# Four changes together in a two-block transformer kernel: opening order, output projections begun inside the attentions, modulation summed by VectorE, copies of transposes moved up

## The chip, the cores and the metric

One core of one Trainium2 chip. The metric is the device time of one execution in microseconds (us). Lower is better.

## What is computed

Two transformer blocks run one after the other on x (512 tokens, 1024 features, fp32). The first block is a gated feed-forward network, an attention with eight banded heads and eight heads that mix three branches (compressed, selected, windowed), and a second feed-forward network. The second block has two layers, both steered by a condition vector c:

```
c_act = silu(c)
mod = c_act @ mod_w[l] + mod_b[l]                    # 1024 x 6144, for l = 0, 1
sh1, sc1, g1, sh2, sc2, g2 = split(mod, 6)
hn = rms_norm(h, norm1_g[l]) * (1 + sc1) + sh1
h = h + g1 * (attention(hn) @ wo)                    # l = 0: chunked, l = 1: latent
hn = rms_norm(h, norm2_g[l]) * (1 + sc2) + sh2
h = h + g2 * conv_ffn(hn)
...
shift, scale = split(c_act @ kv_mod_w + kv_mod_b)    # 1024 x 2048, between the layers
return rms_norm(h, final_g)
```

So the modulation is one vector of 14 panels of 1024 features: 14 matrices of 1024 x 1024 against the one vector c_act.

## The kernel before

Every large product is made of three fp32r matmuls: activation and weight are each split into a high and a low part (hi, lo), and hi*hi, lo*hi and hi*lo are summed in PSUM (`feature_major` L345 to L347 or with the operands' roles kept the other way L339 to L341). A weight chunk of 128 x 2048 is loaded by SP into `raw` (two slots), ScalarE copies it to `w_hi` (`split_hi`, L318), VectorE subtracts to give `w_lo` (`split_lo`, L322), and TensorE uses it. The semaphore `used` frees the slot of hi and lo, `lo_done` that of `raw`. Order on each engine is the order in which the program text calls its functions; there is no scheduler.

The stages, in order of time: ffn1, projection and `att_1`, output projection `out_1`, ffn2, qkv and `att_chunked`, `out_2`, ffn3, latent layer and `att_latent`, `out_3`, ffn4. Ahead of each stage a `Norm` scales the rows of x on VectorE (L609), transposes them on TensorE (L677) into banks, and ScalarE and VectorE take them out as `xT_hi` and `xT_lo` (L625 and L649, or L632 to L660 where a shift is added).

**Opening.** SP issues two rows, the four parts of x, then some 25 small loads of constants (L372), and then the first weight chunk. ScalarE does the norm's squares, the eight `xT_hi`, then the first `w_hi`. VectorE does the scaling, the eight `xT_lo`, the first `w_lo`, and then the constants out of PSUM (banks 5 and 6, L467). TensorE waits for the last `xT_lo`, transposes the constants (L443 to L446), waits for `cols_done`, and starts ffn1.

**Modulation.** GpSimd loads 1024-column rows of a panel, 512 KB each, in four slots (L530), eight to a panel. VectorE multiplies each by its element of c_act, a value per partition, and sums them in `mod_sum` (L544, L546). Then `mod_reduce` (L555) sums over partitions on TensorE with eight matmuls against a column of ones, and `mod_columns` (L561) adds the bias. Ten panels are made beside ffn1, one for two chunks of weights, and four beside the output part of ffn2. The sum is one panel late, so `mod_reduce` stands 15 times.

**Attention.** `PairAttention.pe` runs steps k. In each it issues the scores of k, the products with the values of k-2, and the transposes of the probabilities of k-1 (L1458, L1498, L1480). VectorE adds bias and takes the minimum (L1594), ScalarE takes the exponentials (L1532), VectorE and GpSimd scale by the inverse sums (L1652), and after the transposes ScalarE and VectorE copy banks 4 to 6 into `score` (L1545, L1547), from where the products with the values read. `copies` names who copies which bank: act, dve, act. On ScalarE the copies stand behind all four exponentials of a step, on VectorE behind the scaling. `values_pe` waits for all copies.

**Output projection.** `MixOut` multiplies the attention's result by w_out in two panels of 512 columns, each from two chunks (kt 0 to 3 and 4 to 7), for four groups of 128 tokens s, in banks 4 to 7 for both panels. In the second block, VectorE multiplies by the gate row g1 (L2000) and adds to x (L2003). `Row` makes such a row: eight transposes on TensorE (L1949) into banks 0 and 1, two copies on VectorE (L1955, L1956) into `row`. `row_g1` (g1) is made behind the attention, and TensorE waits for it; `row_g2` (g2, for ffn3) behind `out_2`, and TensorE waits for that ahead of the norm's transposes. The same holds for `row_g3` and `row_g4` in the second layer. Between the panels of `out_2`, VectorE makes the angles of the rotary tables and ScalarE their sine and cosine (`rope_dve`, `rope_act`).

Of the kernel before, what the change touches and what calls it, by code (L numbers as in the profile page):

```python
# [4 lines left out]
P = 128  # L5
# [82 lines left out]
def program(nc, A, strips_dram, skewed, out):  # L88
    stack = ExitStack()
    with stack:  # L90
# [44 lines left out]
        mod_sum = take("mod_sum", [P, MOD])  # L135
# [3 lines left out]
        row = take("row", [P, D])  # L139
        score = take("score", [P, 4, SEQ])  # L140
        probT_at = cursor[0]
        cT = take("cT", [P, 2, SEQ])
        cols = take("cols", [P, 5 * P + 2 * KT])
        mod_cols = take("mod_cols", [P, 15 * KT])
        ident = take("ident", [P, P])
        mean_w = take("mean_w", [P, P])
        ones = take("ones", [P, 1])
# [3 lines left out]
        c_act = take("c_act", [P, KT])  # L151
# [22 lines left out]
        first_rows = take("first_rows", [2 * KT, P], at=work + 12288)  # L174
# [114 lines left out]
        col["ffn1_norm"], col["c"] = FIRST, FIRST + KT  # L289
# [11 lines left out]
        def mod_part(name):  # L301
            k = PANELS[name] + 1
            return mod_cols[:, KT * k:KT * k + KT]
# [52 lines left out]
        in_dma, x_in, first_in, small_in, c_act_done = sem("in_dma"), sem("x_in"), sem("first_in"), sem("small_in"), sem("c_act_done")  # L356
# [9 lines left out]
        def first_load(sp):  # L366
            for n, name in enumerate(("ffn1_norm", "c_2")):
                sp.dma_start(first_rows[n * KT:(n + 1) * KT, :], by_128(A[name][0])).then_inc(first_in, 16)
# [25 lines left out]
        def constants_load_small(pool):  # L394
# [9 lines left out]
            get(cmp_b2v[:, :], A["cmp_b2"][0, 1].partition_broadcast(P))  # L404

# [28 lines left out]
        def first_pe(pe):  # L434
            pe.wait_ge(ident_done, 2)
            pe.wait_ge(first_in, 32)
            pe.transpose(bank[7][:, 0:2 * KT], first_rows[:, :], ident[0:2 * KT, 0:2 * KT]).then_inc(cols_T, 1)

        def constants_pe(pe):
            pe.wait_ge(in_dma, in_dmas[0])  # L440
            pe.wait_ge(edge_zero, ROWS_MADE)
            for b in range(4):
                pe.transpose(bank[5][:, b * P:(b + 1) * P], rows[:, b, :], ident[:, :])  # L443
            pe.transpose(bank[6][:, 0:P], rows[:, 4, :], ident[:, :])
            for kind in range(2):
                last = pe.transpose(bank[6][:, P + kind * CMP_LEN:P + (kind + 1) * CMP_LEN],  # L446
                                    pos_rows[:, kind, :, :].rearrange("p a d -> p (a d)"),
                                    ident[0:CMP_LEN, 0:CMP_LEN])
            last.then_inc(cols_T, 1)

        def first_dve(dve):
# [4 lines left out]
            dve.memset(ones[:, :], 1.0)  # L456
            for n in range(MOD_SLOTS):
                dve.memset(mod_sum[:, n * MOD // MOD_SLOTS:(n + 1) * MOD // MOD_SLOTS], 0.0).then_inc(mod_step, 1)
            dve.memset(mod_cols[:, :], 0.0)
# [3 lines left out]
            dve.tensor_copy(cols[:, FIRST:FIRST + 2 * KT], bank[7][:, 0:2 * KT]).then_inc(cols_done, 1)  # L463

        def constants_dve(dve):
            dve.wait_ge(cols_T, 2)
            dve.tensor_copy(cols[:, 0:4 * P], bank[5][:, :])  # L467
            dve.tensor_copy(cols[:, 4 * P:5 * P], bank[6][:, 0:P])
            dve.tensor_copy(cmp_pos[:, :, :].rearrange("p a b -> p (a b)"),
                            bank[6][:, P:P + 2 * CMP_LEN]).then_inc(cols_done, 1)  # L470
# [33 lines left out]
        def c_act_act(act):  # L504
            act.wait_ge(cols_done, 1)
            act.activation(c_act[:, :], column("c", KT), ACT.Silu).then_inc(c_act_done, 1)


        mod_step, mod_red, mod_ev = sem("mod_step"), sem("mod_red"), sem("mod_ev")
# [9 lines left out]
        def modulation_pool(pool, first, end, strip=None):  # L519

            p0 = 0
            for w in (A["mod_w_2"][0], A["kv_mod_w_2"], A["mod_w_2"][1]):
                n = w.shape[1] // MOD
                lo, hi = max(first - p0, 0), min(end - p0, n)
                if lo < hi:
                    with pool.Fori(0, hi - lo) as p:
                        for kt in range(KT):
# [3 lines left out]
                                           w[kt * P:(kt + 1) * P, bass.ds(MOD * lo + MOD * p, MOD)]).then_inc(mod_ld[kt % MOD_SLOTS], 16)  # L531
# [5 lines left out]
        def mod_steps(dve, k, kts):  # L537

            for kt in kts:
                dve.wait_ge(mod_ld[kt % MOD_SLOTS], 16 * (KT // MOD_SLOTS * k + kt // MOD_SLOTS + 1))  # L540
                dve.wait_ge(mod_step, KT * k + kt + MOD_SLOTS)
                c = c_act[:, kt:kt + 1]
                if kt == 0:
                    ins = dve.tensor_scalar(mod_sum[:, :], mod_rows(0), c, None, ALU.mult)  # L544
                else:
# [4 lines left out]
        def mod_reduce(pe, k, b):  # L550

            pe.wait_ge(mod_step, KT * k + MOD_SLOTS)
            pe.wait_ge(mod_ev, k + 1)
            for t in range(KT):
                last = pe.matmul(bank[b][:, t:t + 1], lhsT=mod_sum[:, t * P:(t + 1) * P], rhs=ones[:, :],  # L555
                                 start=True, stop=True)
            last.then_inc(mod_red, 1)

        def mod_columns(dve, k, b):
            dve.wait_ge(mod_red, k + 1)  # L560
            dve.tensor_tensor(out=mod_cols[:, bass.ds(KT * k, KT)], in0=bank[b][:, 0:KT],  # L561
                              in1=cols[:, bass.ds(KT * k + (col["mod_b"] - KT), KT)], op=ALU.add).then_inc(mod_ev, 1)
# [11 lines left out]
        class Norm:  # L574
# [36 lines left out]
            def act(self, act, gained=None):  # L611

                if not self.again:
                    for s in range(TOK):
                        self.stats_act(act, s)
                if gained is not None:
# [20 lines left out]
            def dve(self, dve, scaled=0):  # L637

                for s in range(scaled, TOK):
                    self.scale_dve(dve, s)  # L640

# [66 lines left out]
        credited = [used, mod_ev, *pair_free, *x_added]  # L708
# [1981 lines left out]
```

## Time and profile before

| what | value |
|---|---|
| median of 3 runs | 2349.35 us (2349.22 to 2352.9) |
| the profiled execution | 2358.37 us |
| its span | 2356.9 us |
| TensorE busy (matmuls) | 2255.7 us, 96% of the span |
| VectorE, ScalarE, GpSimd busy | 54%, 41%, 12% |
| mean granted TensorE clock | 0.976 of full speed |
| DMA | 266.41 MB, mean 113 GB/s |

A profile row of the timeline gives start, duration, engine, source line, operation, and in brackets how long the engine was idle before it and which instruction released it. Matmuls overlap: one of 512 columns is shown with 0.39 us while the next starts 0.23 us after it.

### The profile page before, as it was taken

Reading aid. Unit: us, or ns where it says so; the run is one execution under the profiler, and the core shown is the slowest. Engines: PE = TensorE matmul, PEld = TensorE weight load, DVE = VectorE, ACT = ScalarE, POOL = GpSimd, SP = SyncE. Lnnn points to the kernel's source line nnn. Section 1 sums busy time; section 2 is a strip of 40 time slices with the busy share of each in tenths; the row PEclk is TensorE's granted clock in tenths of the full one; section 3 lists DMA queues with packets and bytes.
Section 4 is the critical chain, followed back from the end, with each engine's and each line's share of the span. In section 5 each row is a group of like instructions: output and inputs, shape, how many; then the busy total and the mean of one; then the engine's idle time right before and its main releaser. Section 6 shows DMA issues by size and latency. Waiting matters only on the chain.

```text
span 2356.9 us, 31898 instructions
## 1 busy us (share of the span) xinstructions
PE 2255.7 (96%) x11876; PEld 1882.9 (80%) x11876; DVE 1273.7 (54%) x1968; ACT 964.1 (41%) x1469; POOL 275.0 (12%) x441
## 2 busy tenths in 40 slices
PE   6999999998899999999999899999989999999998
PEld 5888887896778888888887778888878877888886
DVE  5763763535744344346338566456466656554564
ACT  4322323425735323324228354245244554542542
POOL 2110220013520011001009000000000340000000
PEclk9999999986999999999999999999999999999999
DMA  6863983212022356345321222332312102333322
GB/s 208 262 220 111 284 300 121 72 56 82 28 90 72 89 184 203 85 155 192 106 91 55 76 72 80 108 107 71 116 47 72 55 19 72 89 94 111 89 86 92
DMA packets 258594, 266.41 MB, mean 113 GB/s; under 512 B 8847, under 2 KB 201918, under 8 KB 258510
## 3 DMA queue, kind: packets, MB, share of 16 engines
q1 hardware_dynamic: 236925, 187.20, 26.7%
q0 software_dynamic: 21584, 78.10, 9.7%
q8 instruction: 51, 0.84, 0.1%
q14 instruction: 34, 0.27, 0.0%
HBM read 263.10 MB, written 12.66 MB: 117 GB/s over the span
## 4 chain that ended last, share of the span: by engine, by line
PE 88%; DVE 5%; ACT 4%; issue 1%; SPq 1%; POOL 0%; DMA 0%; DVEq 0%; ACTq 0%; POOLq 0%
PE bank L339 15%; PE bank L341 15%; PE bank L340 15%; PE bank L345 11%; PE bank L347 11%; PE bank L346 11%; PE bank L1458 2%; PE bank L1480 2%; PE bank L1498 2%; ACT probs L1532 2%; PE bank L555 1%; PE bank L677 1%; DVE xT_lo L652 1%; ACT score L1545 1%; DVE probs L1594 1%
## 5 line engine op out<-in xcount | busy, mean ns | idle before, releaser
L322 DVE TENSOR_TENSOR w_lo<-raw,w_hi 128x2048 fp32r<-128x2048 f32 (+3 forms) x202 | 415.3, 2056 | 388.1 <-ACT w_hi L318 387.6
L339 PE MATMUL bank<-xT_hi,w_hi 128*128 128x512 f32 x1552 | 607.4, 391 | 8.1 <-DVE xT_lo L652 4.2
L340 PE MATMUL bank<-xT_lo,w_hi 128*128 128x512 f32 x1552 | 604.5, 390 | 0.0
L341 PE MATMUL bank<-xT_hi,w_lo 128*128 128x512 f32 x1552 | 604.5, 390 | 0.0
L318 ACT ACTIVATE w_hi<-raw 128x2048 fp32r<-128x2048 f32 (+3 forms) x202 | 348.2, 1724 | 498.9 <-PE bank L347 448.5
L339 PEld LDWEIGHTS bank<-xT_hi,w_hi 128*128 128x128 f32 x1552 | 291.9, 188 | 72.0 <-DVE xT_lo L652 8.1
L341 PEld LDWEIGHTS bank<-xT_hi,w_lo 128*128 128x128 f32 x1552 | 291.8, 188 | 61.4
L340 PEld LDWEIGHTS bank<-xT_lo,w_hi 128*128 128x128 f32 x1552 | 292.0, 188 | 59.7
L345 PE MATMUL bank<-w_hi,hid_hi 128*128 128x512 f32 x704 | 274.3, 390 | 0.0
L347 PE MATMUL bank<-w_hi,hid_lo 128*128 128x512 f32 x704 | 273.9, 389 | 0.0
L346 PE MATMUL bank<-w_lo,hid_hi 128*128 128x512 f32 x704 | 273.9, 389 | 0.0
L1652 POOL TENSOR_SCALAR probs<-probs,stat 128x256 f32<-128x256 f32 (+2 forms) x120 | 120.5, 1016 | 739.7 <-DVE stat L1571 711.2
L841 ACT ACTIVATE hid_hi<-act_u 128x512 f32 (+1 forms) x88 | 55.6, 632 | 292.7 <-DVE act_u L900 292.7
L347 PEld LDWEIGHTS bank<-w_hi,hid_lo 128*128 128x128 f32 x704 | 132.2, 188 | 27.6
L345 PEld LDWEIGHTS bank<-w_hi,hid_hi 128*128 128x128 f32 x704 | 132.2, 188 | 27.3
L346 PEld LDWEIGHTS bank<-w_lo,hid_hi 128*128 128x128 f32 x704 | 132.2, 188 | 27.2
L1532 ACT ACTIVATE probs<-probs,small 128x512 f32<-128x512 f32 (+2 forms) x224 | 120.7, 540 | 78.8 <-DVE small L1594 78.8
L345 PE MATMUL bank<-w_hi,xT_hi 128*128 128x512 f32 (+3 forms) x320 | 113.2, 354 | 3.9 <-DVE xT_lo L652 2.9
L346 PE MATMUL bank<-w_lo,xT_hi 128*128 128x512 f32 (+3 forms) x320 | 112.1, 350 | 0.0
L347 PE MATMUL bank<-w_hi,xT_lo 128*128 128x512 f32 (+3 forms) x320 | 112.1, 350 | 0.0
L892 DVE SCALAR_TENSOR_TENSOR act_u<-bank,cols,act_u 128x511 f32<-128x511 f32 x88 | 65.9, 749 | 78.6 <-ACT act_u L833 72.3
L900 DVE TENSOR_TENSOR act_u<-act_g,bank 128x512 f32<-128x512 f32 x44 | 30.2, 687 | 138.2 <-PE bank L341 138.2
(295 smaller groups left out, 2922.9 us busy)
## 6 DMA issues: line engine op xcount, KB each, us to landing
raw<-in_ffn_w_in_dram SPq DMA_DIRECT2D x40, 1024.0 KB, 6.1
raw<-in_f_win_dram SPq DMA_DIRECT2D x40, 1024.0 KB, 6.0
mod_w<-in_mod_w_dram POOLq DMA_DIRECT2D x48, 512.0 KB, 5.5
mod_w_more<-in_mod_w_dram POOLq DMA_DIRECT2D x48, 512.0 KB, 5.9
raw<-in_ffn_w_out_dram SPq DMA_DIRECT2D x24, 768.0 KB, 4.5
raw<-in_f_wout_dram SPq DMA_DIRECT2D x24, 768.0 KB, 4.4
raw<-in_a_wqkv_dram SPq DMA_DIRECT2D x12, 1024.0 KB, 5.1
skewed_strips<-bias_strips POOLq DMA_DIRECT2D x32, 320.0 KB, 6.5
```

The lines of the kernel that those rows point to most:

```text
L318: act.activation(w_hi[:, slot, :n], raw[:, slot, :n], ACT.Copy).then_inc(hi_done, 1)
L322: dve.tensor_tensor(out=w_lo[:, slot, :n], in0=raw[:, slot, :n], in1=w_hi[:, slot, :n].bitcast(f32), op=ALU.subtract).then_inc(lo_done, 1)
L339: pe.matmul(o, lhsT=w[0], rhs=xs[0], start=first, stop=False)
L340: pe.matmul(o, lhsT=w[0], rhs=xs[1], start=False, stop=False)
L341: return pe.matmul(o, lhsT=w[1], rhs=xs[0], start=False, stop=last)
L345: pe.matmul(o, lhsT=xs[0], rhs=w[0], start=first, stop=False)
L346: pe.matmul(o, lhsT=xs[0], rhs=w[1], start=False, stop=False)
L347: return pe.matmul(o, lhsT=xs[1], rhs=w[0], start=False, stop=last)
L841: act.activation(hid_hi[:, bass.ds(k, 1), :].rearrange("p a n -> p (a n)"), act_u[:, u, :], ACT.Copy).then_inc(hid_hi_done, 1)
L892: dve.scalar_tensor_tensor(out=dst[:, u, shift:], in0=bank[b][:, :SEQ - shift], scalar=w, in1=dst[:, u, shift:], op0=ALU.mult, op1=ALU.add ...
L1532: act.activation(p, p, ACT.Exp, scale=-1.0, bias=self.least(k, i), accum_out=self.sums(k, i)).then_inc(self.e, 1)
L1652: return engine.tensor_scalar(p, p, self.inverses(k, i), None, ALU.mult)
```

## The change

1. **Modulation.** The modulation weights are laid out with features first in the host's arrays, so that a load holds 128 output features (partitions) by 1024 inputs. c is loaded to all partitions (`c_row`) and put through silu there. Each of the eight loads of a panel is one fused multiply and sum along the row on VectorE, which gives 128 features. `mod_sum`, `mod_reduce`, its bank and its waits are gone, and `mod_columns` closes each panel.
2. **Opening.** The first weight chunk is issued ahead of the constants, its split stands between the norm's statistics and `xT_hi` (ScalarE), and between scaling and `xT_lo` (VectorE). The constants' transposes use banks 2 and 3 and wait for four `xT_lo`; only the second chunk waits for `cols_done`.
3. **Attention.** ScalarE copies bank 4 between the second and third exponentials, VectorE copies bank 5 ahead of `lo` and scaling; `values_pe` waits for the banks that the next products read.
4. **Output projection.** The first panel goes to banks 0 to 3. Its first chunk for s = 0 is issued in the attention's step N, for s = 1 in step N+1 (N is the number of steps). Gate rows g1 are made in step 1 of the attention, g2 between the panels, both copied by ScalarE, each into a tile of its own.

```diff
         def mod_steps(dve, k, kts):
             for kt in kts:
                 dve.wait_ge(mod_ld[kt % MOD_SLOTS], ...)
-                dve.wait_ge(mod_step, KT * k + kt + MOD_SLOTS)
-                c = c_act[:, kt:kt + 1]
...
-                    ins = dve.scalar_tensor_tensor(out=mod_sum[:, :], in0=mod_rows(kt), scalar=c,
-                                                   in1=mod_sum[:, :], op0=ALU.mult, op1=ALU.add)
-                ins.then_inc(mod_step, 1)
+                tile = mod_rows(kt)
+                dve.tensor_tensor_reduce(out=tile, in0=tile, in1=c_row[:, :], scale=1.0, scalar=0.0, op0=ALU.mult, op1=ALU.add,
+                                         accum_out=mod_dots[:, kt:kt + 1]).then_inc(mod_step, 1)
 
+            def copied(self, pe, k, b):
+                by = self.steps[k].copies[:b + 1]
+                pe.wait_ge(self.pa, self.after("pa", k, by.count("act")))
+                if "dve" in by:
+                    pe.wait_ge(self.pd, self.after("pd", k, by.count("dve")))
...
                         act.activation(self.hi[:, g, :], bank[7][:, :], ACT.Copy).then_inc(self.h, 1)
+                    if 1 <= k <= len(self.steps):
+                        self.copies(act, k - 1, "act", (0,))
                     if step and step.windows is None:
                         self.exps_act(act, k, (2, 3))
...
+                    large = step and step.windows is None and step.sink is None
+                    if large:
+                        dve.wait_ge(self.e, self.after("e", k, 2))
+                        dve.reciprocal(self.inverses(k, 0, 2), self.sums(k, 0, 2)).then_inc(self.r, 1)
+                    if 1 <= k <= len(self.steps):
+                        self.copies(dve, k - 1, "dve")
                     if k - 2 in self.last:
...
+            def beside(self):
+                k = len(self.att.steps)
+                return {k: lambda pe: self.gemm.piece(pe, 0, 0, [0]), k + 1: lambda pe: self.gemm.piece(pe, 0, 0, [1])}
+            def pe(self, pe, between=None):
+                self.gemm.piece(pe, 0, 0, [2, 3])
+                self.gemm.piece(pe, 0, 1, range(TOK))
+                if between:
+                    between(pe)
+                self.gemm.pe(pe, 1)
...
+                def second_free(pe, p, s):
+                    if s == 0 and self.row_between:
+                        self.row_between.done(pe)
+                    if s == TOK - 1:
+                        att.done(pe)
...
             for s in range(TOK):
                 sp.dma_start(x[:, s, :], ...)
+            ffn1.pair_sp(sp, 0, 0, 0)
             constants_load(sp)
...
-            norm_ffn1.act(act)
-            split_hi(act, 2, 0, landed(2))
+            norm_ffn1.act(act, None, lambda act: split_hi(act, 2, 0, landed(2)))
+            c_row_act(act)
```

**Opening on ScalarE.** The end of the norm's statistics, the first `w_hi` and the eight `xT_hi`, before:

```order
L599 ACTIVATE score,small<-x 128x1024 [waits cols_done,x_in]
L601 ACTIVATE small<-small,eps 128x1 [waits norm_ss]
L625 ACTIVATE xT_hi<-bank,zero,cols 128x512 [waits norm_T] x8
L318 ACTIVATE w_hi<-raw 128x2048 [waits raw_landed0]
```

and after:

```order
L585 ACTIVATE score,small<-x 128x1024 [waits cols_done,x_in]
L587 ACTIVATE small<-small,eps 128x1 [waits norm_ss]
L319 ACTIVATE w_hi<-raw 128x2048 [waits raw_landed0]
L613 ACTIVATE xT_hi<-bank,zero,cols 128x512 [waits norm_T] x8
L506 ACT_TABLE_LOAD
L506 ACTIVATE c_row<-c_row 128x1024 [waits cond_in]
```

The first `w_hi` is now ahead of the `xT_hi`, and silu over c stands behind them.

**End of `att_chunked` on TensorE.** `probs` are transposed, `v_*` are the values, `mod_cols` is the gate row, `w_*` by `q_*` is the output projection. Before:

```order
L1480 MATMUL bank<-ident,probs_120 128x128 x10
L1498 MATMUL bank<-score,v_xn 64x128 x4
L1498 MATMUL bank<-score,v_mod 64x128 x2
L1498 MATMUL bank<-score,v_prob 64x128 x2
L1498 MATMUL bank<-score,v_xn 64x128 x2
L1480 MATMUL bank<-ident,probs_120 128x128 x10
L1498 MATMUL bank<-score,v_xn 64x128 x4
L1498 MATMUL bank<-score,v_mod 64x128 x2
L1498 MATMUL bank<-score,v_xn 64x128 x4
L1949 MATMUL bank<-ident,mod_cols 128x128 x8
L345 MATMUL bank<-w_hi,q_hi 128x512
```

and after, where twelve matmuls of the projection stand at each place of which the first is shown:

```order
L1485 MATMUL bank<-ident,probs_121 128x128 x10
L346 MATMUL bank<-w_hi,q_hi 128x512
...
L1510 MATMUL bank<-score,v_xn 64x128 x4
L1510 MATMUL bank<-score,v_mod 64x128 x2
L1510 MATMUL bank<-score,v_prob 64x128 x2
L1510 MATMUL bank<-score,v_xn 64x128 x2
L1485 MATMUL bank<-ident,probs_121 128x128 x10
L346 MATMUL bank<-w_hi,q_hi 128x512
...
L1510 MATMUL bank<-score,v_xn 64x128 x4
L1510 MATMUL bank<-score,v_mod 64x128 x2
L1510 MATMUL bank<-score,v_xn 64x128 x4
```

The gate row has left this place, and two pieces of the projection stand ahead of the last two products with the values.

## Rows read from the trace of the kernel before

**Rows 1.** Page, busy time of engines, and shares of the last chain.

```profile
PE 2255.7 (96%) x11876; PEld 1882.9 (80%) x11876; DVE 1273.7 (54%) x1968; ACT 964.1 (41%) x1469; POOL 275.0 (12%) x441
...
PE 88%; DVE 5%; ACT 4%; issue 1%; SPq 1%; POOL 0%; DMA 0%; DVEq 0%; ACTq 0%; POOLq 0%
```

**Rows 2.** Timeline around one mod_reduce in ffn2; then its line over the whole span.

```profile
851.13 1.84 PE L555 MATMUL bank<-ones,mod_sum 128*128 128x1 f32 x16
852.83 0.49 PE L345 MATMUL bank<-w_hi,hid_hi 128*128 128x512 f32 x1
...
L555 PE MATMUL bank<-ones,mod_sum x240: 164/250/250, 42.7 to 1094.0; 128*128 128x1 f32 x120
```

**Rows 3.** Groups of VectorE by shape: count, busy us, mean ns, idle before.

```profile
L546 DVE SCALAR_TENSOR_TENSOR mod_sum<-mod_w_more,c_act,mod_sum 128x1024 f32<-128x1024 f32 x56 | 71.8, 1283 | 2.1 <-DMA mod_w_more<-in_mod_w_dram 0.6 <-DMA mod_w_more<-in_kv_mod_w_dram 0.2
L544 DVE TENSOR_SCALAR mod_sum<-mod_w,c_act 128x1024 f32<-128x1024 f32 x14 | 10.4, 744 | 0.0
L1594 DVE CUSTOM_DVE_ANT_0 probs<-bank,tables 128x512 f32<-128x512 f32 x32 | 20.6, 682 | 2.0 <-PE bank L1458 1.8
```

**Rows 4.** A stretch of ffn1's second half: us, busy of PE, PEld, DVE, ACT, POOL, PEclk, DMA share, GB/s.

```profile
290.00:314.00 24.00, 24.00 (x115) 20.14 (x114) 16.72 (x15) 8.76 (x8) 6.57 (x14) 1.00 1.01 337
```

**Rows 5.** Timeline of the opening.

```profile
16.41 0.29 ACT L601 ACTIVATE small<-small,eps 128x1 f32<-128x1 f32 x1
...
19.08 5.43 DVE L649 SCALAR_TENSOR_TENSOR xT_lo<-bank,cols,xT_hi 128x512 fp32r<-128x512 f32 x8 [1.38 <-ACT xT_hi L625]
...
24.57 1.11 PE L443 MATMUL bank<-ident,rows 128*128 128x128 f32 x4 [3.46 <-DVE xT_lo L649]
...
30.20 0.77 PE L339 MATMUL bank<-xT_hi,w_hi 128*128 128x512 f32 x1 [3.95 <-DVE cmp_pos L469]
```

**Rows 6.** Chain of the opening: start, us, what.

```profile
15.52 8.70 DMA raw<-in_ffn_w_in_dram
...
26.18 2.29 DVE w_lo L322
```

**Rows 7.** TensorE in att_1: a group of heads, and its end.

```profile
616.45 0.77 PE L1775 MATMUL bank<-score,cmp_vz 128*64 128x128 f32 x10 [0.83 <-ACT score L1545]
...
620.68 0.55 PE L1498 MATMUL bank<-score,v_tok 128*64 128x128 f32 x6 [0.72 <-ACT score L1545]
...
671.13 1.31 PE L1498 MATMUL bank<-score,v_tok 128*64 128x128 f32 x20 [0.69 <-ACT score L1545]
```

**Rows 8.** TensorE in and behind att_chunked, up to out_2's last chunk.

```profile
1291.68 0.66 PE L1498 MATMUL bank<-score,v_xn 128*64 128x128 f32 x8 [0.40 <-ACT score L1545]
...
1299.58 0.66 PE L1498 MATMUL bank<-score,v_xn 128*64 128x128 f32 x8 [1.55 <-DVE score L1547]
...
1302.97 0.66 PE L1498 MATMUL bank<-score,v_xn 128*64 128x128 f32 x8 [0.69 <-ACT score L1545]
...
1306.92 0.50 PE L345 MATMUL bank<-w_hi,q_hi 128*128 128x512 f32 x1 [1.63 <-DVE row L1956]
...
1341.69 0.50 PE L345 MATMUL bank<-w_hi,q_hi 128*128 128x512 f32 x1 [1.83 <-DVE w_lo L322]
```

**Rows 9.** From the end of out_2 to the first column taken out for ffn3.

```profile
1352.71 1.03 PE L1949 MATMUL bank<-ident,mod_cols 128*128 128x128 f32 x8
...
1358.34 0.78 ACT L632 ACTIVATE full<-bank,mod_cols,gain 128x512 f32<-128x512 f32 x1 [2.50 <-PE bank L677]
```

**Rows 10.** End of att_latent, first matmul of out_3, first column taken out for ffn4.

```profile
1923.94 1.31 PE L1498 MATMUL bank<-score,v_all 128*64 128x128 f32 x20 [1.65 <-DVE score L1547]
...
1931.29 0.50 PE L345 MATMUL bank<-w_hi,q_hi 128*128 128x512 f32 x1 [1.63 <-DVE row L1956]
...
1974.95 1.03 PE L1949 MATMUL bank<-ident,mod_cols 128*128 128x128 f32 x8
...
1982.44 0.78 ACT L632 ACTIVATE full<-bank,mod_cols,gain 128x512 f32<-128x512 f32 x1 [3.74 <-PE bank L677]
```

**Rows 11.** The stretch of projection and early att_1, columns as in rows 4.

```profile
518.00:565.00 47.00, 40.10 (x214) 36.51 (x214) 18.46 (x69) 18.12 (x52) 21.27 (x30) 0.50 0.27 80
```

More of the change, by code:

```diff
@@ L999, in pe, with piece @@
             def pe(self, pe, p):
+                for i in range(len(self.panels[p][1])):
+                    self.piece(pe, p, i, range(TOK))
+            def piece(self, pe, p, i, ss):
                 n, kts, _, c0 = self.panels[p]
-                if p == 0:
+                if p == 0 and i == 0 and 0 in ss:
                     self.ready(pe)
-                at, total = 0, sum(kts)
-                for c, m in enumerate(kts, c0):
-                    pe.wait_ge(lo_done, c + 1)
+                total = sum(kts)
+                for c, m in ((c0 + i, kts[i]),):
+                    at = sum(kts[:i])
+                    if 0 in ss:
+                        pe.wait_ge(lo_done, c + 1)
                     lo, width = 0, n
@@ L1533, in exps_act, with copies @@
                                    accum_out=self.sums(k, i)).then_inc(self.e, 1)
-            def copies(self, engine, k, name):
-                step, done = self.steps[k], 0
+            def copies(self, engine, k, name, banks=(0, 1, 2)):
+                step = self.steps[k]
                 for b, by in enumerate(step.copies):
-                    if by != name:
+                    if by != name or b not in banks:
                         continue
@@ L1988, in dve @@
             def dve(self, dve, norm, between=None):
+                if self.gate is not None:
+                    self.gate.done(dve)
                 for p in range(2):
@@ L2487, in program @@
         latent = LatentLayer(norm_kv, norm_q)
-        row_g3 = Row("g1_1", lambda pe: None, 0)
+        row_g3 = Row("g1_1", 5, row_mid)
         out_3 = MixOut(A["b_wo_2"][0], att_latent, row_g3, q2_hi, q2_lo)
         norm_ffn4 = modulated_norm(4, out_3.x_ready)
-        row_g4 = Row("g2_1", row_g3.done, 0)
-        ffn4 = Ffn(A["f_win_2"][1], A["f_wout_2"][1], norm_ffn4, conv=1, row_gate=True)
+        row_g4 = Row("g2_1", 6, row)
+        ffn4 = Ffn(A["f_win_2"][1], A["f_wout_2"][1], norm_ffn4, conv=1, row_gate=row_g4)
         norm_final = Norm(ffn4.x_ready)
+        att_chunked.banks_free, att_latent.banks_free = row_g1.done, row_g3.done
+        out_2.row_between, out_3.row_between = row_g2, row_g4
         final_c = chunks.take(1)
@@ L2645, in _ @@
             qkv.done(pe)
-            att_chunked.pe(pe)
-            row_g1.pe(pe)
-            out_2.pe(pe)
-            row_g2.pe(pe)
-            row_g2.done(pe)
+            att_chunked.pe(pe, {1: row_g1.pe, **out_2.beside()})
+            out_2.pe(pe, row_g2.pe)
             norm_ffn3.pe(pe)
```

258 lines of the change are left out of this document (123 added, 135 removed).

## The prediction

> **What bounds the kernel now.** The page comes first. TensorE is busy for 96% of the span and is 88% of the chain that ended last [rows 1]. Work on VectorE, ScalarE or GpSimd therefore counts only where TensorE stands still for it, and the kernel gets shorter in two ways: less work on TensorE, or a smaller gap on it. TensorE's timeline tells where the gaps are. Within the four feed-forward stages none is over 0.35 us; they lie in the opening [rows 5], inside the attentions at the copies of transposes [rows 7, 8], and around the output projections [rows 8 to 10]. The profiled execution took 2358.37 us against a median of 2349.35. I form the sum as a difference and take it off the median.
>
> **Modulation, TensorE.** One `mod_reduce` delays the next product from 851.13 to 852.83 [rows 2]: 1.70 us, and the matmul behind it is some 0.1 longer than its like (0.49 instead of 0.39, half of which I count); I take 1.75. The line has 240 matmuls of 16 a call [rows 2], hence 15 calls. Fourteen stand in the middle of products: 14 x 1.75 = 24.5. The last, from 1094.0, stands beside VectorE's work on the norm, which TensorE awaits in any case; I give it 0.5. Gain 25.0, and since this is issued work that vanishes, no cover is needed.
>
> **Modulation, VectorE.** Before, a panel is one L544 and seven L546: 0.744 + 7 x 1.283 = 9.73 us [rows 3]. After, it is eight fused sums of 128x1024, each with a read of the accumulator. The trace has no such operation with both sources in SBUF. The nearest rows are L1594, 682 ns for 512 columns with one source in PSUM, and L546, 1283 ns for 1024 columns with two in SBUF. Twice the first is 1.36, the second 1.28. I take 1.3, that is 10.4 us a panel (9.6 to 11). VectorE is busy 16.72 of 24 us there [rows 4], so 0.7 more finds room. This costs nothing.
>
> **Modulation, DMA.** In the second half of ffn1 the queues are already full: share 1.01, 337 GB/s [rows 4]. A panel moves about 7.6 MB (4.2 of modulation, 2.1 of weights, 1.3 of strips, by the shapes). TensorE's 96 matmuls at 0.2275 us are 21.9 us, and before, with the reduction, 23.6. So the queues must give 347 GB/s where they gave 322. The loads become runs of whole rows, which should not hurt. I take a loss of 1.0, from 0 to 6, the latter if all five panels of this half stay at 23 us.
>
> **Opening.** TensorE's first product starts at 30.20 [rows 5]. Its chain was the weights landing at 24.2, `w_hi` up to 26.18 (1.9), `w_lo` 2.29 [rows 6]; the first of these DMAs had stood behind the constants. Moved ahead, the load should be there at about 16, when the statistics end (16.7) [rows 5]. Then `w_hi` runs to 18.6, `w_lo` to 20.9, and the eight `xT_lo`, 5.43 us in all or 0.68 each, follow; the fourth is done at 23.6. The transposes of the constants take 1.1 and with their small ones 1.7 [rows 5]; the first product starts at 25.3. That is 4.9 earlier. Bounds are 2, if the weights land at 19 because x and they share the queues, and 6. What was on the path and is hidden now is the copy of constants (3.95 idle before 30.20). Silu over `c_row` is behind `xT_hi` and delays only the first modulation sums.
>
> **Copies of transposes.** In att_1 a group of heads has gaps of 0.83 and 0.72 that end with ScalarE's copy L1545 [rows 7]. Bank 4 was transposed well before, and the copy stood behind two more exponentials, so moving it up frees the first. There are three such groups, 4.65 us, and two first ones and three banded steps with larger gaps at the same line. Some remain, since other banks are still copied behind all exponentials, and everything behind the moved copy, exponentials 2 and 3 and then scaling, comes 0.6 later. I take 5.0, from 0 to 9.5. In att_chunked the gap is 0.40 a step [rows 8], six times: 2.4, from 0 to 3.5. att_latent waits for nothing: 0. The gap of 0.69 at att_1's end [rows 7] is covered by a piece of the projection: 0.7, from 0 to 1.75, since two smaller ones stand behind it.
>
> **out_2.** Three terms.
> - Start. At att_chunked's end TensorE waits 1.55 and 0.69 for copies and 1.63 for the gate row [rows 8], and spends 1.09 on its transposes. A piece of the projection is twelve matmuls, 2.75 us, so it covers each of the first two; the row is made in step 1 of the attention, in a gap of 1.2 there. 1.55 + 0.69 + 1.63 + 1.09 = 4.96; I take 4.9.
> - Between the panels. Row g2 now stands here: transposes 1.03 [rows 9], then two ScalarE copies that TensorE waits for, 1.35 (by L632, 0.78 for 512 columns [rows 9], a little less when only copied). 2.38 are added. The gap of 1.83 before the second chunk [rows 8] goes, since the wait comes earlier. Loss 0.55.
> - End. Before, `row_g2`'s transposes from 1352.71, the wait for VectorE's copies, the norm's transposes, and the first column taken out at 1358.34 [rows 9]: 5.63 after the last product. Without the row, the last addition, scaling and transposes remain, about 4.5. Gain 1.1.
>
> Together 4.9 - 0.55 + 1.1 = 5.45.
>
> **out_3.** The same with the same lines: the start has 1.65 for a copy and 1.63 for the row [rows 10], 0.69 and 1.09 as in out_2, thus 5.05. Between the panels 2.38 is lost and nothing goes. At the end the row costs more (7.49 from 1974.95 to 1982.44 [rows 10] against about 5.2), a gain of 2.2. Sum 4.9. Both together range from 5 to 12.
>
> **Sum.** 25.0 - 1.0 + 4.9 + 5.0 + 2.4 + 0.7 + 5.45 + 4.9 = 47.35. Off the median of 2349.35 this is 2302.0, and I write **2302**. The clock adds noise: TensorE ran at 0.50 from 518 to 565 [rows 11], behind a stretch in which it waited, and 40.10 us busy there are worth 20 at full clock. Such stretches shift with every gap; I allow 4 either way.
>
> **Rivals.**
> - **The fused sum runs at half speed** (the other side). Should a sum with two SBUF sources and an accumulator take twice L1594's doubled rate with its read, 2.56 us, a panel would take 20.5 us plus 9.3 of VectorE's other work and waits (16.72 of 24 us less 9.73, and two waits for TensorE of about 1): 29.8 instead of 23.6. Ten panels of ffn1 would cost 62 instead of giving 17.5, and the four beside ffn2's outputs another 18. The time would be 2302 + 80 + 17 = about 2399. VectorE becomes the bound from about 1.6 us a sum on ((21.9 - 9.3) / 8), and the total is slower than before from about 2.2 on, where ten panels cost 47 more. Against it: L546 has two SBUF sources in fp32 and takes 1283 ns for 1024, so two sources alone do not halve the rate [rows 3]. For it: no row has two sources and an accumulator. Chance 0.05.
> - The Trainium skill, "Vector Engine (DVE) Microarchitecture Reference", section "7. Points that are easy to get wrong", says that a scalar-tensor-tensor operation with two non-bf16 SBUF sources halves its throughput, as both read ports are used and none is left to read back the accumulator. By that rule this rival is the result. The trace agrees in no row; L546, of the form it names, is not halved.
> - **ffn1's second half is bound by its DMAs.** Share 1.01 [rows 4] speaks for it, against it that 337 GB/s is close to the 347 wanted. The five panels keep 23 us: 5 to 6 less, 2307. Chance 0.15.
> - **The attentions give nothing.** The copies move ahead of work that ends last, the pieces of the projection only move the gap behind them, and the rows' copies wait longer between the panels. Then 5.0, 2.4 and 0.7 go and half of 10.35: 2302 + 8.1 + 5.2 = 2315. Chance 0.17.
> - **The opening gives 2 or less**, because the weights' DMAs run beside x and both land late: 2305 to 2307. Chance 0.13.
>
> **Chances.** The forecast as summed, with its small errors, has 0.50, the four rivals 0.05, 0.15, 0.17 and 0.13. With all gaps at their best ends, the time is 2290; with DMA and attentions both bad, 2321. The range 2288 to 2320 leaves out the half-speed sum and about 0.1 more. A measurement of this kernel can tell 0.2%, 4.7 us, from no change. Faster by more than that 0.93, within it 0.02, slower 0.05.
>
> **What would show it.** `mod_reduce` has no line; TensorE's busy time is lower by about 26 us. The fused sum's mean is 1.2 to 1.4 us; at 2.2 or more, with gaps in ffn1 that end on `w_lo`, the first rival holds. In ffn1's second half no TensorE gap ends on `raw`'s DMA. TensorE's first product starts near 25.3. No gap over 0.5 stands before L1510's values at the attentions' ends. Between out_2's panels stands a gap of about 1.35 that ScalarE's copy ends. I am wrong if the gaps in the attentions have gone to other waiters (scaling, exponentials), or if a stage that was full before shows new gaps.

## The result

| kernel | median | ratio to before, 95% interval |
|---|---|---|
| before | 2351.12 us (2349.22 to 2354.24, 4 runs) | |
| changed | 2322.43 us (2320.83 to 2328.03, 4 runs) | 0.9872 [0.9856, 0.9889] |

The change gives 28.7 us. 47.35 were forecast, with 2302 as the time and 2288 to 2320 as the range; the time lies outside it. The profiled execution of the changed kernel took 2320.83 us, its span 2319.3.

The page of the changed kernel, busy time of the engines:

```profile
PE 2237.0 (96%) x11636; PEld 1848.1 (80%) x11636; DVE 1269.3 (55%) x2068; ACT 949.3 (41%) x1462; POOL 266.7 (12%) x442
```

Against [rows 1] the 240 matmuls of `mod_reduce` are gone (11876 to 11636). They held 27.6 us of busy time, yet TensorE's busy time fell by 18.7 only, where the prediction named about 26 as a sign. A clock that was granted more often (0.981 of full in the mean, 0.976 before) should have made it fall further. That is the first sign: something that stayed takes longer. The stage table says where. It gives how far ahead of the kernel before the changed one is at the same product (from the start times in the two traces):

| at | changed | after_p128, below |
|---|---|---|
| ffn1's first product | 5.3 | 5.1 |
| ffn1's last | 18.1 | 23.2 |
| out_1's last | 27.5 | 34.9 |
| ffn2's last | 31.8 | 44.0 |
| out_2's last | 37.0 | 51.1 |
| ffn3's last | 34.4 | 51.4 |
| out_3's last | 38.6 | 56.0 |
| ffn4's last | 37.6 | 58.2 |

The trace of the kernel before is of an execution that took 2358.37 us, 7 to 9 above its medians, with more time at half clock between ffn1's last product and out_1's; so from out_1 on both columns are several us too large, and the steps from row to row say more than the last row.

ffn3 and ffn4 hold nothing that the change moved, and the changed kernel loses 2.6 and 1.0 us in these rows. Within ffn4, from its first product behind the norm on, it loses 2.4, and its two groups of output products take 1.5 more each. Neither stage has a gap over 0.35 us on TensorE in its products. The loss is in the pitch, the time from one matmul's start to the next.

To read the rows that follow, one must know the roles of the operands. The kernel's text has the weight as `lhsT`, the operand that stands still (stationary), in `feature_major` (L339 to L341), where xT moves past it; `token_major` (L345 to L347) holds hid (or q) stationary and moves the weight. The rows of the profile name the moving operand first: L339 has `xT_hi,w_hi`, L345 has `w_hi,hid_hi`. The description of the kernel ahead gives the two line ranges the other way round, and the expectation for w_p128 below calls xT stationary in the 1552 triples of L339, where it moves.

TensorE's timeline in the output products of ffn1, of the kernel before:

```profile
379.62 0.39 PE L346 MATMUL bank<-w_lo,hid_hi 128*128 128x512 f32 x1
379.85 0.39 PE L347 MATMUL bank<-w_hi,hid_lo 128*128 128x512 f32 x1
380.08 0.39 PE L345 MATMUL bank<-w_hi,hid_hi 128*128 128x512 f32 x1
380.30 0.39 PE L346 MATMUL bank<-w_lo,hid_hi 128*128 128x512 f32 x1
380.53 0.39 PE L347 MATMUL bank<-w_hi,hid_lo 128*128 128x512 f32 x1
380.76 0.39 PE L345 MATMUL bank<-w_hi,hid_hi 128*128 128x512 f32 x1
380.98 0.39 PE L346 MATMUL bank<-w_lo,hid_hi 128*128 128x512 f32 x1
```

and of the changed kernel, the same instructions:

```profile
380.76 0.39 PE L346 MATMUL bank<-w_hi,hid_hi 128*128 128x512 f32 x1
380.99 0.39 PE L347 MATMUL bank<-w_lo,hid_hi 128*128 128x512 f32 x1
381.23 0.39 PE L348 MATMUL bank<-w_hi,hid_lo 128*128 128x512 f32 x1
381.45 0.39 PE L346 MATMUL bank<-w_hi,hid_hi 128*128 128x512 f32 x1
381.68 0.40 PE L347 MATMUL bank<-w_lo,hid_hi 128*128 128x512 f32 x1
381.92 0.40 PE L348 MATMUL bank<-w_hi,hid_lo 128*128 128x512 f32 x1
382.16 0.40 PE L346 MATMUL bank<-w_hi,hid_hi 128*128 128x512 f32 x1
```

Six steps take 1.36 us before and 1.40 after. Over all 2112 such matmuls the mean is 226.8 ns before and 232.4 after; the products with w stationary and xT moving keep 226.9. No row of waits shows it: the views that group by stretch call both engines full. A stretch of 35 us in those products, before (us, then busy of PE, PEld, DVE, ACT, POOL, PEclk, DMA share, GB/s):

```profile
370.00:405.00 35.00, 35.00 (x156) 28.97 (x155) 11.75 (x10) 9.18 (x6) 0.00 (x0) 1.00 0.35 111
```

and changed:

```profile
352.00:387.00 35.00, 35.00 (x152) 28.40 (x151) 12.01 (x10) 9.44 (x7) 0.00 (x0) 1.00 0.34 105
```

Both are 35.00 busy at full clock, with 156 matmuls in one and 152 in the other. 704 triples x 3 x 5.6 ns is 12 us. The matmuls of out_1 and out_2 (384, 5.4 to 6.3 ns more each) add 2, and those with w stationary and `lat` moving in the latent layer (144, 227.0 to 233.3 ns) almost 1: 15 in all. The expectations below leave the last group out and say 14.

What differs for these matmuls is an address. The change makes `cols` and `mod_cols` 32 bytes shorter each and drops `ones`. With the rounding of tiles to 128 bytes, everything from `small` on, and with it the working area that holds hid, q and k, lies 128 bytes lower in each partition of SBUF. Before, hid_hi and w_hi were a multiple of 512 bytes apart (162432 - 90240 = 141 x 512); now they are 128 less.

### The profile page after: what moved, and what is told of

The parts are those of the page before. It is cut to its first block, busy times and chain, and to the rows that moved or that the text cites. A ratio compares the mean times of both kernels' runs of the same rounds, so it can differ in the third digit from the quotient of the medians.

```text
span 2319.3 us, 31376 instructions
## 1 busy us (share of the span) xinstructions
PE 2237.0 (96%) x11636; PEld 1848.1 (80%) x11636; DVE 1269.3 (55%) x2068; ACT 949.3 (41%) x1462; POOL 266.7 (12%) x442
## 4 chain that ended last, share of the span: by engine, by line
PE 88%; DVE 5%; ACT 4%; POOL 1%; issue 1%; DMA 1%; DVEq 0%; SPq 0%; ACTq 0%; POOLq 0%
PE bank L340 15%; PE bank L341 15%; PE bank L342 15%; PE bank L346 11%; PE bank L348 11%; PE bank L347 11%; PE bank L1461 2%; PE bank L1510 2%; PE bank L1485 2%; ACT probs L1546 1%; POOL probs L1668 1%; PE bank L667 1%; DVE w_lo L323 1%; DVE xT_lo L642 1%; DVE probs L1610 0%
## 5 line engine op out<-in xcount | busy, mean ns | idle before, releaser
L341 PE MATMUL bank<-xT_lo,w_hi 128*128 128x512 f32 x1552 | 604.9, 390 | 0.0
L341 PEld LDWEIGHTS bank<-xT_lo,w_hi 128*128 128x128 f32 x1552 | 292.2, 188 | 59.8
L347 PE MATMUL bank<-w_lo,hid_hi 128*128 128x512 f32 x704 | 277.8, 395 | 0.0
L1668 POOL TENSOR_SCALAR probs<-probs,stat 128x256 f32<-128x256 f32 (+2 forms) x120 | 113.9, 960 | 737.3 <-DVE stat L1581 703.0
L347 PEld LDWEIGHTS bank<-w_lo,hid_hi 128*128 128x128 f32 x704 | 132.6, 188 | 30.8
L347 PE MATMUL bank<-w_lo,xT_hi 128*128 128x512 f32 (+3 forms) x320 | 111.8, 349 | 0.0
L901 DVE TENSOR_TENSOR hid_lo<-act_u,hid_hi 128x512 f32 (+1 forms) x88 | 61.0, 693 | 76.0 <-ACT hid_hi L836 76.0
```

The lines of the kernel that those rows point to most:

```text
L341: pe.matmul(o, lhsT=w[0], rhs=xs[1], start=False, stop=False)
L347: pe.matmul(o, lhsT=xs[0], rhs=w[1], start=False, stop=False)
L901: dve.tensor_tensor(out=hid[1], in0=act_u[:, u, :], in1=hid[0].bitcast(f32), op=ALU.subtract).then_inc(pair_free[u], 1)
L1668: return engine.tensor_scalar(p, p, self.inverses(k, i), None, ALU.mult)
```

## The experiments

### The working area back at its place, and the kernel before moved

after_p128 and after_all128 are the changed kernel with one edit each, w_p128 is after_p128 with one more, and before_m128 is the kernel before with one; after_p256 and after_p384 add 256 and 384 where after_p128 adds 128.

```diff
 after_p128
-        work = cursor[0] = (cursor[0] + LINE - 1) // LINE * LINE
+        work = cursor[0] = (cursor[0] + LINE - 1) // LINE * LINE + 128
 after_all128
-        cursor = [(nc.sbuf_base + LINE - 1) // LINE * LINE]
+        cursor = [(nc.sbuf_base + LINE - 1) // LINE * LINE + LINE]
 w_p128
+        cursor[0] += LINE
         raw = take("raw", [P, 2, CHUNK])
 before_m128
-        c_act = take("c_act", [P, KT])
...
         late_rows = take("late_rows", [P, 1])
+        c_act = take("c_act", [P, KT])
```

> The changed kernel, with only the working area (hid, q, k) placed 128 bytes further on in SBUF, where it lay before the change. Address theory: a matmul of 512 columns with its stationary operand in hid starts every 226.7 ns as in the kernel before, not every 232.4 ns; 704 triples x 17 ns = 12.0 us, with out_1 (64 x 20 ns = 1.3) and out_2 (about 0.7) come back, so about 14 us below the changed kernel, near 2308. Rival (the stretch comes from the changed order, the queues or the new loads, not from the address): 232.4 ns stays, and the time is that of the changed kernel, near 2322.

> The kernel before, with only the working area 128 bytes lower in SBUF (c_act is placed in a hole behind late_rows, which lets all behind it move down). Address theory: the output products slow from 226.7 to 232.4 ns a matmul, and the kernel takes 14 us more than before, near 2364. Rival (the stretch comes with the other edits): 226.7 ns stays, 2350.

> The changed kernel with its working area 256 bytes further on. Tells which offsets are slow: if only the changed kernel's place is bad (an offset of 0 to a 512-byte line, with the moving w_hi at 128), this one shows 226.7 ns; if only the place of before is good (same offset as w_hi), it shows more than 226.7 ns. I expect 226.7.

> The changed kernel with every tile 128 bytes further on, so that hid stands at the absolute place of before while its distance to w_hi stays that of the changed kernel. If the absolute place decides, the pitch is 226.7 ns and the time about 14 us below the changed kernel; if the distance between stationary and moving operand decides, the pitch stays 232.4 ns. I lean to the distance, 6 to 4.

> The changed kernel with its working area 384 bytes further on, so that hid lies 256 bytes from a multiple of 512 bytes away from w_hi. If the distance must be a multiple of 512, output products start every 232.4 ns; if a multiple of 256 is enough, every 226.7 ns. I lean to 256 being enough, 5 to 5 on what is shown so far.

> As after_p128, with raw, w_hi, w_lo and everything behind them 128 bytes further on, x and xT where they were. hid and w_hi keep their distance, a multiple of 512 bytes; xT and w_hi are now 128 off. If the distance between the two operands decides, the output products stay at 226.7 ns and those with xT stationary (1552 triples) slow to 232.4 ns: 1552 x 17 = 26 us more, about 2330. If something about the working area itself decides, xT's products stay at 226.7 ns and the time at 2304.

| kernel | hid from w_hi, mod 512 | xT from w_hi, mod 512 | pitch, hid | pitch, xT | time |
|---|---|---|---|---|---|
| before | 0 | 0 | 226.8 ns | 226.9 ns | 2351.12 |
| changed | 384 | 0 | 232.4 | 226.9 | 2322.43 |
| after_p128 | 0 | 0 | 226.7 | 226.8 | 2303.72, ratio 0.979 [0.9774, 0.9807] |
| before_m128 | 384 | 0 | 232.4 | 226.9 | 2365.77, ratio 1.005 [1.0033, 1.0067] |
| after_p256 | 128 | 0 | 232.4 | 226.8 | 2314.5, one run |
| after_all128 | 384 | 0 | 232.4 | 226.8 | 2319.91, one run |
| after_p384 | 256 | 0 | 226.7 | 226.8 | 2305.25, one run |
| w_p128 | 0 | 384 | 226.8 | 233.0 | 2334.81, one run |

The same stretch of after_p128, columns as above:

```profile
348.00:383.00 35.00, 35.00 (x156) 28.98 (x155) 12.97 (x10) 10.38 (x8) 0.00 (x0) 1.00 0.33 105
```

The address theory holds on both sides: the place alone makes the changed kernel faster and the kernel before slower, by 12.6 us (7.8 to 15.8 by the ratio's interval) where 14 were expected. after_p256 went against what I expected, after_all128 with it: the absolute place does not decide (128 mod 512 is good for hid in before and bad in after_all128), the distance between the stationary and the moving operand does. after_p384 shows that a multiple of 256 bytes is enough. w_p128 is the strongest: it has nothing to do with the change, and there the products that were never slow become slow, while hid stays good. TensorE's timeline of w_p128 in ffn1's second half, where six steps take 1.39 us:

```profile
329.67 0.39 PE L341 MATMUL bank<-xT_hi,w_hi 128*128 128x512 f32 x1
329.89 0.40 PE L342 MATMUL bank<-xT_lo,w_hi 128*128 128x512 f32 x1
330.13 0.39 PE L343 MATMUL bank<-xT_hi,w_lo 128*128 128x512 f32 x1
330.36 0.40 PE L341 MATMUL bank<-xT_hi,w_hi 128*128 128x512 f32 x1
330.60 0.39 PE L342 MATMUL bank<-xT_lo,w_hi 128*128 128x512 f32 x1
330.83 0.40 PE L343 MATMUL bank<-xT_hi,w_lo 128*128 128x512 f32 x1
331.06 0.39 PE L341 MATMUL bank<-xT_hi,w_hi 128*128 128x512 f32 x1
```

1552 triples x 3 x 6.2 ns are 29 us; the time is 31 above after_p128, one run. These are the products with w stationary and xT moving. Those with xT stationary and w moving (475 pitches of 512 columns, most in the projections) slow too, from 226.8 to 232.5 ns at full clock, which adds near 3. So either role may hold either tile.

### Whether the place is all

> The changed kernel as it is, on the same chip and in the same rounds as p128_same. The pitch of the matmuls explains 14 us between the two, the medians so far, from different jobs, stand 18.7 apart. If the rest was the clock and the chip of those jobs, the two stand 12 to 16 apart here, with this one near 2317; if the place costs something else too, 18 or more, with this one near 2322.

> The changed kernel with its working area 128 bytes further on, the same program as after_p128: 2302 to 2306, a ratio to before of 0.979 to 0.980.

In the same rounds, after_same took 2318.78 us (2316.73 to 2321.06), ratio 0.9853 [0.9838, 0.9869]; p128_same 2301.70 (2300.52 to 2310.44), ratio 0.9799 [0.9779, 0.9819]. The medians stand 17.1 apart, the ratios 12.7, and the pitch explains 15. The rest of the 18.7 that lie between the medians of the first measurements is within what single kernels scatter: the five runs of p128_same go from 2300.52 at a mean granted clock of 0.985 to 2310.44 at 0.981. So the pitch explains what the place costs, about 15 us; a second cost of a few us would hide in this scatter, and none is shown.

### The parts one by one

Each of these starts from after_p128, so that the place is good. A difference "by the ratios" is taken between two ratios to the kernel before, each with an interval of some 4 us either way, so it is uncertain by about 6. after_p128 and p128_same are one program and have 0.9790 and 0.9799: with the second, each loss below is 2.1 us smaller.

copies_back puts the copies back:

```diff
-                    if 1 <= k <= len(self.steps):
-                        self.copies(act, k - 1, "act", (0,))
...
-                        self.copies(act, k - 1, "act", (1, 2))
+                        self.copies(act, k - 1, "act")
...
-                    if 1 <= k <= len(self.steps):
-                        self.copies(dve, k - 1, "dve")
                     if k - 2 in self.last:
...
                         self.scaled_dve(dve, k, 1)
+                    if 1 <= k <= len(self.steps):
+                        self.copies(dve, k - 1, "dve")
```

> As after_p128, with ScalarE's copies of bank 4 back behind all four exponentials and VectorE's copy of bank 5 back behind lo and scaling, while the projection's pieces, rows, opening and modulation stay changed. By the prediction's terms (5.0 in att_1 and 2.4 in att_chunked) this costs 7.4 us against after_p128: about 2311; the part of the ends is covered by the pieces in any case. Rival (the copies give nothing, their gaps move to other waiters): 2304.

It took 2312.68 us, ratio 0.9824 [0.9804, 0.9843], 8.0 by the ratios against 7.4 (5.9 from p128_same). The gaps of [rows 7] are back; TensorE in a group of att_1:

```profile
594.89 0.55 PE L1788 MATMUL bank<-score,cmp_vz 128*64 128x128 f32 x6 [0.84 <-ACT score L1557]
```

lo_first puts VectorE's `lo` ahead of its copy and leaves the rest:

```diff
-                    if 1 <= k <= len(self.steps):
-                        self.copies(dve, k - 1, "dve")
                     if k - 2 in self.last:
...
                                           op=ALU.subtract).then_inc(self.l, 1)
+                    if 1 <= k <= len(self.steps):
+                        self.copies(dve, k - 1, "dve")
```

> The changed kernel at the good place (as after_p128), with VectorE's steps of an attention ordered reciprocal, lo, copy of bank 5, scaling, where the change has reciprocal, copy, lo, scaling. The trace of the changed kernel has a gap of 0.8 us that ends with q_lo at the start of four groups of att_1, and 1.2 at one more. Theory: the copy (0.69) stands between q_hi and q_lo and is what TensorE waits for, so the gap falls to 0.1 to 0.3 and the time by 2 to 4 us against after_p128 (2304 to 2301). Rival: the second half of the products then waits for the copy of bank 5 instead, the gap only moves, and the time stays within 1 us.

My theory fell. In the changed kernel a group waits for `q_lo`:

```profile
595.26 0.98 PE L1510 MATMUL bank<-score,v_tok 128*64 128x128 f32 x14 [0.81 <-DVE q_lo L1587]
```

and in lo_first for the copy:

```profile
598.15 0.66 PE L1510 MATMUL bank<-score,v_tok 128*64 128x128 f32 x8 [1.17 <-DVE score L1561]
```

The products need both, and `lo` waits for ScalarE's `hi` as well, so the copy behind it comes later still. It took 2307.69 us, ratio 0.9805 [0.9787, 0.9824], no faster than after_p128. In att_1, VectorE's copy ends 5.0 us of TensorE's idle time, where `q_lo` ended 4.6 in after_p128: the gap only moved.

opening_back issues the constants first again, and puts the splits and TensorE's waits back:

```diff
-            ffn1.pair_sp(sp, 0, 0, 0)
             constants_load(sp)
-            ffn1.sp(sp, True)
+            ffn1.sp(sp)
...
-            norm_ffn1.part(pe, 3)
+            norm_ffn1.done(pe)
             constants_pe(pe)
+            pe.wait_ge(cols_done, 2)
```

> As after_p128, with the first weight chunk issued behind the constants again, its split behind xT_hi and xT_lo, and TensorE waiting for all xT_lo and for the constants ahead of ffn1. By the prediction's term 4.9 us are lost, 5.5 by the traces: about 2309, with TensorE's first product near 30.4. Rival: other work behind silu over c or the modulation's loads hides a part of it, and the loss is under 3.

It took 2310.74 us, ratio 0.9819 [0.98, 0.9838]: 6.8 by the ratios (4.7 from p128_same). TensorE's first product starts at 31.52 instead of 25.07, 6.45 later, and 1.3 later than in the kernel before. The first weight chunk takes 10.48 us from issue to landing where the kernel before had 8.70 [rows 6]; mod_only shows the same, 9.87 us and a first product at 31.00. Both have the old order beside a new load, that of `c_row`, which GpSimd issues at 10.4 ahead of the first modulation loads. That this load is the cause is likely, but no run leaves it out.

outs_back takes `TokenGemm.pe`, `MixOut` and `Row` from the kernel before, with their calls; mod_only is outs_back with the edits of copies_back and opening_back too, so that of the four parts only the modulation is left.

```diff
-            att_chunked.pe(pe, {1: row_g1.pe, **out_2.beside()})
-            out_2.pe(pe, row_g2.pe)
+            att_chunked.pe(pe)
+            row_g1.pe(pe)
+            out_2.pe(pe)
+            row_g2.pe(pe)
+            row_g2.done(pe)
```

> As after_p128, with the output projections as before: both panels in banks 4 to 7, nothing of them in the attentions, the gate rows behind the attention and behind the projection, copied by VectorE, and TensorE waiting for each. By the prediction's terms (0.7 + 5.45 + 4.9) 11 us are lost: about 2315. Since the copies of transposes are moved up here, the waits of 1.55 and 1.65 for them may be smaller than in the kernel before, then the loss is 8 to 9, 2312. Rival: the pieces only cover what something else makes late, the loss is under 4.

> The kernel before with the modulation of the change alone (opening order, copies and projections as before), its working area at the good place. By the prediction 25.0 - 1.0 = 24 us less than before; by the traces 15 x 1.75 without a loss to the DMAs, 25: about 2328. Rival: c_row's load, its silu or the denser loads take something back, then it is 18 to 20 less.

outs_back took 2318.72 us, ratio 0.9848 [0.9828, 0.9868], 13.6 by the ratios against 11. mod_only took 2327.95, ratio 0.9898 [0.988, 0.9917], 24.0 below before, against 24 forecast. The four parts add up to 24.0 + 6.8 + 8.0 + 13.6 = 52.4 where the whole gives 49.4; with p128_same they are 24.0 + 4.7 + 5.9 + 11.5 = 46.1 where the whole gives 47.3. The parts account for the whole, but with uncertainties of 4 to 6 us each they can't tell a term of 5 from one of 8.

## Why the prediction was wrong, point by point

**The sum.** Forecast were 47.35; at the good place 49.4 were measured (2353.14 - 2303.72) and, by the ratio of p128_same, 47.3. So the terms together were right within the noise for a kernel whose tiles stay where they were. The step that failed is none of them but one that was put at nothing without a word: that the matmuls which the change leaves alone keep their pitch. The change moves the working area by 128 bytes against w_hi, and 2112 output products take 5.6 ns more each, and those of out_1, out_2 and `lat` in the latent layer about as much each. Of the 20.4 us by which 2322.43 misses 2302, 15 are this. The rest is not traced to anything: the kernel before was 1.8 us slower here than the median that the sum was taken off, and after_same, the same program as the changed kernel, is at 2318.78. The prediction's sign for such a case, that a stage which was full before shows new gaps, could not catch it: ffn3 and ffn4 got longer without a gap.

**Modulation.** Forecast were 25.0 on TensorE less 1.0 lost to the DMAs; mod_only gives 24.0, within 4 either way. VectorE's fused sum:

```profile
L542 DVE CUSTOM_DVE_ANT_0 mod_w_more<-mod_w_more,c_row 128x1024 f32<-128x1024 f32 x56 | 67.7, 1220 | 9.5 <-DMA mod_w_more<-in_mod_w_dram 7.2 <-DMA mod_w_more<-in_kv_mod_w_dram 2.3
...
L542 DVE DVE_READ_ACCUMULATOR2_ANT mod_dots<- 128x1 f32 x112 | 9.2, 82 | 0.0
```

1220 + 82 ns is 1.30, the value taken from [rows 3]. The half-speed rival is out. The Trainium skill, "Vector Engine (DVE) Microarchitecture Reference", section "7. Points that are easy to get wrong", says that S2S2D2_STT with two non-bf16 SBUF sources halves its throughput, for want of a port to read back the accumulator. The halving that the rival priced, 2.56 us a sum, does not show for this fused sum, whose form the trace calls by another name: two fp32 sources in SBUF with an accumulator run 1024 columns in 1220 ns, less than the 1283 of L546 without one. But the prediction held L546 only against L1594, which reads PSUM. Against L544 of [rows 3], one source in SBUF and 744 ns for 1024 columns, both forms with two sources take 1.6 to 1.7 times as long, and no run here tells which rate the halving is meant against.

**DMA.** The rival "bound by its DMAs" is out too. A stretch of ffn1's second half in the changed kernel, columns as above:

```profile
272.00:296.00 24.00, 24.00 (x107) 19.87 (x107) 18.69 (x26) 6.24 (x6) 6.39 (x12) 1.00 1.03 347
```

The queues give 347 GB/s, just what was asked, where [rows 4] had 337, and TensorE has no gap there. The term of 1.0 was nevertheless about right, by a chain that the prediction did not write out. In the changed kernel a modulation load lands late in ffn1, VectorE waits for it ahead of the sum, its next `w_lo` comes late, and TensorE waits for that:

```profile
56.43 1.23 DVE L542 CUSTOM_DVE_ANT_0 mod_w_more<-mod_w_more,c_row 128x1024 f32<-128x1024 f32 x1 [2.63 <-DMA mod_w_more<-in_mod_w_dram]
...
58.41 2.29 DVE L323 TENSOR_TENSOR w_lo<-raw,w_hi 128x2048 fp32r<-128x2048 f32 x1 [0.36 <-issue]
...
60.99 0.47 PE L340 MATMUL bank<-xT_hi,w_hi 128*128 128x512 f32 x1 [1.10 <-DVE w_lo L323]
```

The kernel before has no such gap in ffn1. The changed kernel has 1.1 us of them, after_p128 0.3, the same program as p128_same 1.0, and the other kernels with this modulation from 0 to 2.6. In after_p128 ffn1 ends 23.2 ahead, 5.1 of it from the opening, so nearly the full 10 x 1.75 arrives; in p128_same it ends 21.8 ahead with 5.5 from the opening.

**Opening.** The chain of the changed kernel:

```profile
16.10 1.81 ACT w_hi L319
...
17.93 2.29 DVE w_lo L323
20.23 2.65 DVE xT_lo L639 x4
...
23.33 1.09 PE bank L445 x4
```

Forecast were 16.7 for the start of `w_hi`, 18.6 and 20.9 for its end and that of `w_lo`, and 23.6 for the fourth `xT_lo`, which ends at 22.9. The first product starts at 24.91 instead of 25.3. The term of 4.9 was 5.1 to 5.3 in the traces against the kernel before; the weights had landed in time. opening_back's 6.45 in the trace is more because there the first weights land later than in the kernel before.

**Copies.** 7.4 forecast, 8.0 or 5.9 measured, uncertain by 6. The gaps that ended with ScalarE's copy, 9.5 us in att_1 and 2.8 in att_chunked of copies_back, are gone in after_p128. In att_chunked it is all gain (idle 3.5 against 0.6). In att_1 most of it went to other waiters, which the prediction had named as a sign of being wrong: `q_lo` ends 4.6 us of idle time and GpSimd's scaling 3.7 where it had 1.0, so TensorE's idle time there falls by 2.9 only, from 13.2 to 10.3, where 5.0 were forecast. From its first product with the values to its last the stage is shorter by 6.6 (120.3 against 126.9), part of which is a lower clock in copies_back (0.91 against 0.95); the two can't be told apart here. The waits for `q_lo` were to be seen in the order of the change: VectorE's copy of 0.69 now stands ahead of `lo`.

**Projections.** 11.05 forecast, 13.6 or 11.5 measured, the interval covers all. The waits of 1.55, 0.69 and 1.63 at att_chunked's end [rows 8] are gone. Between the panels of out_2 TensorE waits as forecast, for ScalarE's second copy:

```profile
1293.31 0.47 PE L346 MATMUL bank<-w_hi,q_hi 128*128 128x512 f32 x1 [1.27 <-ACT row_early L1971]
```

1.27 against 1.35. In step 1 of att_chunked the first transposes now wait for the copies of the row, since they use its banks, and a gap stands there that the prediction had not named:

```profile
1208.54 0.66 PE L1485 MATMUL bank<-ident,probs 128*128 128x128 f32 x4 [1.53 <-ACT row L1971]
```

It costs nothing all the same: from att_chunked's first scores to those of its next step it is 6.99 us in after_p128 with the row and 7.09 in outs_back without it, where waits of 1.23 ahead of the scores and of 0.52 and 0.78 for the scaled probabilities fill the same time. The row was free, as forecast. What was off is the end of out_2: from the last product's end by the pitch (1315.68) to the first column taken out (1320.85) it takes 5.17, not 4.5. At out_3 it is 5.43, 2.06 less than in [rows 10], where 2.2 were forecast.

**Clock.** Of the stretch of projection and att_1 from 490 to 600, the kernel before shows

```profile
490.00:600.00 110.00, 95.05 (x694) 85.31 (x692) 52.18 (x194) 52.26 (x151) 39.48 (x57) 0.75 0.22 68
```

and the changed kernel

```profile
490.00:600.00 110.00, 93.64 (x812) 80.42 (x813) 65.31 (x249) 65.11 (x197) 51.61 (x80) 0.83 0.18 54
```

A mean clock of 0.75 over 110 us is some 55 us at half of full speed, one of 0.83 some 37; lo_first and copies_back show 0.75 there as well. That is 17 us more of half clock in the kernel before, worth up to 9 (an estimate: half of 17). The executions of the kernel before show the same link over the whole span, 2348.92 us at a mean clock of 0.980 and 2358.36 at 0.976; that this stretch is what puts the profiled one (2358.37) above its median is likely, but no second trace of that kernel was kept. Why the clock differs between executions stays open. Taking the sum off the median was right for this; the 4 us allowed for it were on the small side for single executions.

## What to carry to other kernels

When an edit adds, drops or shrinks a tile, write out the addresses of everything behind it, and compare the distance between the two operands of each large matmul before and after. Where it is no longer a multiple of 256 bytes (0 and 256 modulo 512 were good here, 128 and 384 bad), price the matmuls anew, or pad. A full engine is not a sum of fixed durations: when a stage that the change doesn't touch gets longer without a gap, count its instructions in a stretch of equal length. The changed kernel with 128 bytes of padding is the fastest here, 2303.72 us against 2322.43 and 2351.12.

## What the runs showed of the hardware that was not expected

At full granted clock, an fp32r matmul of 512 columns with a 128x128 stationary operand starts every 226.7 to 226.9 ns where the two operands lie a multiple of 256 bytes apart in their partitions, and every 232.4 to 233.0 ns where they lie 128 bytes off that. Distances of 0, 128, 256 and 384 modulo 512 were tried; others were not, nor other types. Narrower matmuls show little: in w_p128 those of xT and w with 384 columns go from 174.2 to 176.7 ns and those with 256 from 122.0 to 120.8. That the two reads of SBUF get in each other's way is a guess that no view of the trace shows; what it is in the chip stays open. The durations of single matmuls hide it (0.39 or 0.40 in both cases), and so do the busy times.
